# Cross-attention with folded key and value matrices, and rewritten passes of the conv mixer, in an eight-core decoder trunk

## The reference

```python
D_MODEL = 1024; BATCH = 16; SEQ = 2048; DEPTH = 2; MEM_LEN = 256
HGRN_HEADS = 8; CONV_WIDTH = 31; XATTN_HEADS = 4; XATTN_DIM = 256; D_FF = 2816

def conformer_conv_mixer(h, w_in, b_in, dw, dw_b, ln_g, ln_b, w_out, b_out):
    a, gate = jnp.split(h @ w_in + b_in, 2, axis=-1)
    u = a * jax.nn.sigmoid(gate)
    u = lax.conv_general_dilated(u, dw[:, None, :], ...) + dw_b   # depthwise, causal, width 31
    u = jax.nn.silu(layer_norm(u, ln_g, ln_b))
    return u @ w_out + b_out

def memory_cross_attention(h, mem_n, wq, wkv, wo):
    q = (h @ wq).reshape(B, S, XATTN_HEADS, XATTN_DIM)
    k, v = jnp.split(mem_n @ wkv, 2, axis=-1)
    s = jnp.einsum('bshd,bmhd->bhsm', q, k).astype(jnp.float32) * (XATTN_DIM ** -0.5)
    p = jax.nn.softmax(s, axis=-1).astype(v.dtype)
    o = jnp.einsum('bhsm,bmhd->bshd', p, v).reshape(B, S, D)
    return o @ wo

def reference(...):
    mem_n = rms_norm(mem, mem_norm)                      # shared by both layers
    h = x
    for layer in range(DEPTH):
        h = h + 0.5 * swiglu_ffn(rms_norm(h, ffn1_norm[layer]), ffn1_w_in[layer], ffn1_w_out[layer])
        hn = rms_norm(h, mix_norm[layer])
        h = h + (hgrn2_mixer(hn, ...) if layer == 0 else conformer_conv_mixer(hn, ...))
        h = h + memory_cross_attention(rms_norm(h, xattn_norm[layer]), mem_n, xattn_wq[layer], xattn_wkv[layer], xattn_wo[layer])
        h = h + 0.5 * swiglu_ffn(rms_norm(h, ffn2_norm[layer]), ffn2_w_in[layer], ffn2_w_out[layer])
    return rms_norm(h, final_norm)
```

## Time and profile before

| | |
|---|---|
| median of 3 runs | 6222.91 us (6216.97 to 6978.02) |
| the profiled execution, its time | 6235.01 us |
| its span, slowest core (core 4) | 6233.5 us |
| spans of the eight cores | 6202.5 to 6233.5 us |
| mean granted TensorE clock, core 4 | 0.962 |

### The profile page before, as it was taken

One profiled execution on the slowest core, in us unless ns is written; L12 is line 12 of the kernel. 1 busy time (PEld: TensorE's weight loads), 2 busy tenths in 40 slices (PEclk: granted clock), 3 DMA queues, 4 the chain that ended last, 5 costly groups with the idle time before them and its releaser, 6 DMA issues.

```text
span 6233.5 us, 88931 instructions; the slowest of 8 cores (6202.5 to 6233.5 us)
## 1 busy us (share of the span) xinstructions
PE 5689.4 (91%) x31032; PEld 2786.8 (45%) x31600; DVE 3170.8 (51%) x4054; ACT 2118.9 (34%) x3223; POOL 965.9 (15%) x828
## 2 busy tenths in 40 slices
PE   8899988999999867899989999889999998688999
PEld 3345543444444444344444455434444445443443
DVE  4336565544534556644553465564344445656434
ACT  3118883211311344311331288632122122543113
POOL 2102440000000441000000034200000014400000
PEclk9999999999999988999999999999999999899998
...
GB/s 127 53 26 25 27 26 57 54 34 41 47 33 10 38 45 75 24 48 35 94 103 32 27 26 27 49 47 41 41 40 44 30 6 46 45 65 38 31 31 55
DMA packets 442111, 271.58 MB, mean 44 GB/s; under 512 B 179280, under 2 KB 404560, under 8 KB 441680
## 3 DMA queue, kind: packets, MB, share of 16 engines
...
## 4 chain that ended last, share of the span: by engine, by line
PE 82%; issue 6%; DVE 5%; ACT 3%; DMA 2%; POOL 2%; SPq 1%; DVEq 0%; ACTq 0%; POOLq 0%
PE ps L646 38%; PE ps L661 19%; PE ps L753 4%; PE ps L740 4%; PE ps L1005 3%; PE ps L855 3%; PE ps L957 2%; PE ps L566 2%; PE ps L1094 2%; DVE hn_tok L562 1%; PE ps L883 1%; PE ps L1026 1%; DVE arena L776 1%; PE ps L766 1%; DMA arena<-conv_dw 1%
## 5 line engine op out<-in xcount | busy, mean ns | idle before, releaser
L646 PE MATMUL ps<-arena 128*128 128x512 bf16 x11021 | 2498.8, 383 | 29.6 <-DVE arena L776 10.5
L646 PEld LDWEIGHTS ps<-arena 128*128 128x128 bf16 x11264 | 1107.2, 99 | 1360.0 <-issue 102.1
L649 DVE TENSOR_TENSOR arena<-ps,arena 128x512 bf16<-128x512 f32 x704 | 486.3, 691 | 1801.4 <-PE ps L646 1776.4
L648 ACT ACTIVATE arena<-ps 128x512 bf16<-128x512 f32 x704 | 420.0, 597 | 2754.5 <-PE ps L646 2739.3
L661 PE MATMUL ps<-arena 128*128 128x512 bf16 x5516 | 1255.1, 381 | 14.8 <-DVE h L663 5.7
L663 DVE SCALAR_TENSOR_TENSOR h<-ps,h 128x512 f32<-128x512 f32 x1536 | 1044.1, 689 | 229.8 <-PE ps L661 223.5
L661 PEld LDWEIGHTS ps<-arena 128*128 128x128 bf16 x5632 | 550.5, 98 | 685.0 <-issue 55.2
L593 POOL DMA_DIRECT2D arena<-ffn_w_in x176 | 154.9, 884 | 2407.8 <-PE ps L646 1862.4
L538 ACT ACTIVATE junk<-h 128x1024 bf16<-128x1024 f32 x288 | 303.5, 1054 | 332.9 <-DVE h L596 198.0
L1005 PE MATMUL ps<-arena 128*128 128x512 bf16 x1475 | 368.0, 386 | 3.2 <-issue 0.2
L562 DVE SCALAR_TENSOR_TENSOR hn_tok<-h,stat,gB 128x1024 bf16<-128x1024 f32 x256 | 359.4, 1451 | 20.4 <-PE ps L566 15.1
...
## 6 DMA issues: line engine op xcount, KB each, us to landing
arena<-ffn_w_in POOLq DMA_DIRECT2D x176, 512.0 KB, 8.9
arena<-ffn_w_out POOLq DMA_DIRECT2D x88, 512.0 KB, 6.9
...
y<-arena SPq DMA_DIRECT2D x32, 512.0 KB, 3.5
h<-x SPq DMA_DIRECT2D x20, 512.0 KB, 6.3
...
```

The source lines that it names most:

```text
L646: P.op("pe", lambda e, bb=bb, ga=ga, k=k, j=j: e.matmul(psb(bb), lhsT=wiv[:, ga, k, j * 128:(j + 1) * 128], rhs=hnT[:, k, blk * 512:(blk + ...
L648: P.op("act", lambda e, bg=bg, j=j: e.activation(out=sg[j].ap, in_=psb(bg), func=AF.Silu), reads=psk(bg), writes=sg[j].keys())
L649: P.op("dve", lambda e, bu=bu, j=j, q=q: e.tensor_tensor(out=actv[:, q, :], in0=psb(bu), in1=sg[j].ap, op=ALU.mult), reads=psk(bu) + sg[j] ...
```

## The change

The scores (h Wq)(M Wk)^T of a head are h times a 1024x256 matrix Wq (M Wk)^T, and the output P (M Wv) Wo is P times a 256x1024 matrix. Both matrices depend on layer, sequence and head alone. They are now made once, for both layers and both sequences, in 16 steps (`fold_steps`) recorded at steps 7 to 22 of the very first feed-forward, whose rings shrink from 5 and 5 slots to 3 and 4; they are written to HBM as bf16 through SP's queue and read back by each cross-attention. A step for keys has 4 x 8 matmuls of 256 columns that project the memory, 16 transposes of Wq and 32 matmuls of 256 columns; a step for values has 32 matmuls of 256 columns and 16 of 512. Cross-attention then goes by tiles of 128 tokens: `weigh` (16 matmuls of 512 columns, tokens on partitions, row maximum by `tensor_reduce`, four Exp with bias and sum, one product with the reciprocals), and two tiles later `mix` (8 transposes of the weights, a ScalarE copy, 16 matmuls of 512 columns). `middle` is recorded after step 4, once, for both sequences' memory tokens; the vectors come in rows and are transposed, and the depthwise weights in one load.

In the conv mixer the right operand of the projections is read with a step of 4 tokens, so that the VectorE operation writes without a step; bands and the bias on `h` move from POOL to VectorE; the statistics are split in three; all four classes are scaled on VectorE; and a product with a shifted selection matrix `spread` (32 matmuls of 512 columns a block) takes the place of the 32 transposes and interleaves the classes, so that the copies out of PSUM are contiguous, half on ScalarE, half on VectorE.

```diff
+        P.op("pe", lambda e: e.transpose(out=ps[:, P.place[bv], 0:40], in_=vrow[0:40, :], identity=identf[0:40, 0:40]), reads=vrow_buf.keys() + [("vrow", i) for i in range(4)] + idf_buf.keys(), writes=psk(bv))
...
+            P.op("pool", lambda e: e.dma_start(out=dwtok, in_=cv_dw_d[0]), reads=["tick"], writes=dwtok_buf.keys(), dma=True)
+            P.op("dve", lambda e: e.tensor_copy(out=dwrep, in_=dwtok.rearrange("p (g c) -> p g c", c=32)[:, :, None, :].to_broadcast([CW, D // 32, 4, 32])), reads=dwtok_buf.keys(), writes=dwrep_buf.keys())
...
-            NW, NO, NA = 5, 5, 3
+            NW, NO, NA = (5, 5, 3) if middle is None else (3, 4, 3)
...
-            for g in range(1, NW):
+            for g in range(1, max(NW, NO)):
-                load_wi(g, late)
+                if g < NW:
+                    load_wi(g, late)
...
-                if middle is not None and i == 2 * NB:
+                if middle is not None and i == 4:
                     middle()
+                if steps and i >= 7:
+                    steps.pop(0)()
...
-        def emit_xattn(layer, hook):
...
+        def mem_norms():
...
+        def fold_steps(fw, wqT, kvT, st):
...
+            def project(s, scale):
+                for j in range(2):
+                    for k in range(KC):
+                        P.op("pe", lambda e, k=k, j=j: e.matmul(ps[:, P.place[b], j * 256:(j + 1) * 256], lhsT=wkv_[0][:, k, j * 128:(j + 1) * 128], rhs=mv[:, k, :], start=(k == 0), stop=(k == KC - 1)),
+                P.op("act", lambda e: e.activation(out=kvv[s], in_=psb(b).rearrange("p (j m) -> p j m", m=MEM), func=AF.Copy, scale=scale), reads=psk(b), writes=kvT[s].keys())
...
+            def keys_step(l, hh):
+                wload(wkv_[0], xa_wkv_d[l][:, hh * 256:(hh + 1) * 256].rearrange("(k p) n -> p k n", p=128), fw[0].keys())
+                wload(wkv_[1], xa_wq_d[l][:, hh * 256:(hh + 1) * 256].rearrange("(k p) n -> p k n", p=128), fw[1].keys())
+                for s in range(NSEQ):
+                    project(s, float(256 ** -0.5))
+                for j in range(2):
                     b = P.bank()
                     for k in range(KC):
+                        P.op("pe", lambda e, k=k, j=j, b=b: e.transpose(out=psb16(b)[:, k * 128:(k + 1) * 128], in_=wkv_[1][:, k, j * 128:(j + 1) * 128], identity=ident[:]), reads=fw[1].keys() + ["ident"], writes=psk(b))
...
+                                P.op("pe", lambda e, k=k, i=i, j=j, b=b, s=s: e.matmul(ps[:, P.place[b], i * 256:(i + 1) * 256], lhsT=wqTv[:, j, k * 128:(k + 1) * 128], rhs=kvv[s][:, j, :], start=(j == 0), stop=(j == 1)),
...
+                    P.op("sp", lambda e, s=s, sv=sv: e.dma_start(out=fa_d[l, s, :, :, hh * 256:(hh + 1) * 256], in_=sv), reads=st[s].keys(), writes=[("fa", l, s, hh)], dma=True)
...
+            def values_step(l, hh):
+                wload(wkv_[0], xa_wkv_d[l][:, D + hh * 256:D + (hh + 1) * 256].rearrange("(k p) n -> p k n", p=128), fw[0].keys())
+                wload(wov, xa_wo_d[l][hh * 256:(hh + 1) * 256, :].rearrange("(j p) n -> p j n", p=128), fw[1].keys())
+                for s in range(NSEQ):
+                    project(s, 1.0)
...
+                                P.op("pe", lambda e, mt=mt, half=half, j=j, b=b, s=s: e.matmul(psb(b), lhsT=kvv[s][:, j, mt * 128:(mt + 1) * 128], rhs=wov[:, j, half * 512:(half + 1) * 512], start=(j == 0), stop=(j == 1)),
...
+                    P.op("sp", lambda e, s=s, sv=sv: e.dma_start(out=fv_d[l, s, :, 2 * hh:2 * hh + 2, :], in_=sv), reads=st[s].keys(), writes=[("fv", l, s, hh)], dma=True)
+            return [lambda l=l, hh=hh, f=f: f(l, hh) for l in range(2) for hh in range(4) for f in (keys_step, values_step)]
...
+        def emit_xattn(layer, sq, hook):
+            offs = ((0, 42, 58), (16, 32, 48))[layer]
+            A = ABuf(arena, HNT_B + offs[0] * 1024, KC * D, BF16)
+            VW = ABuf(arena, HNT_B + offs[1] * 1024, KC * D, BF16)
+            CV.off = HNT_B + offs[2] * 1024
+            ex = [CV.take(D, F32) for _ in range(2)]
+            pn = [CV.take(D, BF16) for _ in range(3)]
+            pT = [CV.take(D, BF16) for _ in range(3)]
...
+            for k in range(0, KC, 4):
+                P.op("sp", lambda e, k=k: e.dma_start(out=Av[:, k:k + 4, :], in_=fa_d[layer, sq, :, k:k + 4, :]), reads=[("fa", layer, sq, hh) for hh in range(4)], writes=A.keys(k * D, (k + 4) * D), dma=True)
...
+            def weigh(tt):
+                x, z = tt % 2, tt % 3
+                exv = ex[x].ap.rearrange("p (h m) -> p h m", m=MEM)
+                for hf in range(2):
+                    for k in range(KC):
+                        P.op("pe", lambda e, k=k, hf=hf, b=b: e.matmul(psb(b), lhsT=hnT[:, k, tt * 128:(tt + 1) * 128], rhs=Av[:, k, hf * 512:(hf + 1) * 512], start=(k == 0), stop=(k == KC - 1)),
+                    P.op("dve", lambda e, hf=hf, b=b: e.tensor_reduce(out=xst[:, z, 0, 2 * hf:2 * hf + 2], in_=psb(b).rearrange("p (h m) -> p h m", m=MEM), op=ALU.max, axis=AX.X, negate=True), reads=psk(b), writes=[("xmax", z, hf)])
+                    for i in range(2):
+                        hh = 2 * hf + i
+                        P.op("act", lambda e, hh=hh, i=i, b=b: e.activation(out=exv[:, hh, :], in_=ps[:, P.place[b], i * 256:(i + 1) * 256], func=AF.Exp, bias=xst[:, z, 0, hh:hh + 1], accum_out=xst[:, z, 1, hh:hh + 1]),
+                P.op("dve", lambda e: e.reciprocal(out=xst[:, z, 2, :], in_=xst[:, z, 1, :]), reads=[("xsum", z, hh) for hh in range(4)], writes=[("xrec", z)])
+                P.op("dve", lambda e: e.tensor_tensor(out=pn[z].ap.rearrange("p (h m) -> p h m", m=MEM), in0=exv, in1=xst[:, z, 2, :, None].to_broadcast([128, 4, MEM]), op=ALU.mult), reads=ex[x].keys() + [("xrec", z)], writes=pn[z].keys())
...
+            def mix(tt):
+                for i in range(KC):
+                    P.op("pe", lambda e, i=i, b=b: e.transpose(out=psb16(b)[:, i * 128:(i + 1) * 128], in_=pn[z].ap[:, i * 128:(i + 1) * 128], identity=ident[:]), reads=pn[z].keys() + ["ident"], writes=psk(b))
+                P.op("act", lambda e, b=b: e.activation(out=pT[z].ap, in_=psb16(b), func=AF.Copy), reads=psk(b), writes=pT[z].keys())
+                    for i in range(KC):
+                        P.op("pe", lambda e, i=i, half=half, bo=bo: e.matmul(psb(bo), lhsT=pT[z].ap[:, i * 128:(i + 1) * 128], rhs=VWv[:, i, half * 512:(half + 1) * 512], start=(i == 0), stop=(i == KC - 1)),
+                    add_to_h(tt, half, bo)
+            for tt in range(NT + 2):
+                if tt < NT:
+                    weigh(tt)
+                if tt >= 2:
+                    mix(tt - 2)
+                    if (tt - 2) % 4 == 3:
+                        hook((tt - 2) // 4)
...
+            def y_of(b, q):
+                if q == 0:
+                    return y
+                return ABuf(arena, HNT_B + (b * 4 + (0, 0, 0, 1)[q]) * 4096 + (0, 0, 2048, 0)[q], D, BF16)
...
-                P.op("pool", lambda e: e.tensor_tensor(out=h[:, tt, :], in0=h[:, tt, :], in1=gB[:, gn, :], op=ALU.add), reads=[("h", tt), ("gB", gn)], writes=[("h", tt)])
+                P.op("dve", lambda e: e.tensor_tensor(out=h[:, tt, :], in0=h[:, tt, :], in1=gB[:, gn, :], op=ALU.add), reads=[("h", tt), ("gB", gn)], writes=[("h", tt)])
...
-                            P.op("pe", lambda e, bb=bb, a=a, k=k, v=v, blk=blk: e.matmul(psb(bb), lhsT=v[:, a, k, :], rhs=hnT[:, k, blk * 512:(blk + 1) * 512], start=(k == 0), stop=(k == KC - 1)),
+                            P.op("pe", lambda e, bb=bb, a=a, k=k, v=v, blk=blk: e.matmul(psb(bb), lhsT=v[:, a, k, :], rhs=hnT[:, k, blk * 512:(blk + 1) * 512].rearrange("p (t q) -> p q t", q=4), start=(k == 0), stop=(k == KC - 1)),
...
-                    P.op("dve", lambda e, ba=ba, s=s, c=c, blk=blk: e.scalar_tensor_tensor(out=uTv[:, :, blk * 128:(blk + 1) * 128].rearrange("p q t -> p t q"), in0=psb(ba).rearrange("p (t q) -> p t q", q=4), scalar=vecs[:, V_BA, c:c + 1], in1=sg[s].ap.rearrange("p (t q) -> p t q", q=4), op0=ALU.add, op1=ALU.mult),
+                    P.op("dve", lambda e, ba=ba, s=s, c=c, blk=blk: e.scalar_tensor_tensor(out=uTv[:, :, blk * 128:(blk + 1) * 128], in0=psb(ba).rearrange("p (q t) -> p q t", q=4), scalar=vecs[:, V_BA, c:c + 1], in1=sg[s].ap.rearrange("p (q t) -> p q t", q=4), op0=ALU.add, op1=ALU.mult),
...
-                P.op("pool", lambda e: e.tensor_tensor(out=v, in0=mask32[:, None, :].to_broadcast([128, 36, 32]), in1=dwS[:, gi, :, None].to_broadcast([128, 36, 32]), op=ALU.mult),
+                P.op("dve", lambda e: e.tensor_tensor(out=v, in0=mask32[:, None, :].to_broadcast([128, 36, 32]), in1=dwS[:, gi, :, None].to_broadcast([128, 36, 32]), op=ALU.mult),
...
+            cuts = (0, 512, 768, D)
...
-                if c == 5:
+                if c in (3, 5):
                     for b in range(NB):
-                        stats(b, 0)
+                        stats(b, c // 5)
...
-                for q in (2, 0, 3, 1):
+                for q in range(4):
...
```

(21 more changed lines are left out.)

255 lines of the change are left out of this document (98 added, 157 removed).

## The result

The changed kernel takes 0.9736 of the time of the one before, 95% interval 0.9708 to 0.9764, so it is 2.6% faster; the forecast of 6033 us against 6222.9 was a ratio of 0.9695. In some executions of either kernel the cores of one die or both are granted a lower clock and the time grows by some per cent; these make the plain medians of this comparison 6172.34 us (6055.7 to 6941.49, 4 runs) and 6481.65 us, and are left out of the ratio and of all that follows. Without them the changed kernel took 6054.45, 6055.70 and 6057.36 us; the last is the profiled execution (span 6055.7 us on core 3, clock 0.986).

What follows compares the result with a forecast made beforehand. TensorE, busy 5689 of 6233.5 us, was taken as the bound; -165 - 56 + 123 - 20 - 12 - 60 = -190 us on 6235.0 gave 6045, less 12 for the median 6033 us, range 5965 to 6150.

Steps and rivals of the forecast that it cites:

- Part 1: Cross-attention's PE work: 736 units become 512 plus 128 transposes' 7.2 us, 41.2 us less a stage, -165 us over four.
- Part 2: Cross-attention's gaps, where PE stands: 14 us a stage in place of 28, -56 us (bounds -96 to 0).
- part 5: Conv mixer's main part: contiguous VectorE write, bands and bias on VectorE shrink gaps, -12 us (-30 to +15).
- two tiles of lead: Cross-attention: two `weigh` tiles, 6.9 us, cover the chain of maximum, Exp, reciprocal and product, some 4.5 us.
- Parts 3 and 4: Fold in the first feed-forward, +123 us; depthwise weights in one load ending PE's wait, -20 us.
- Rival (c): Fold stalls the first feed-forward, each of 16 steps waiting 8.9 us for a load: +142, 6175 us; chance 0.10.
- Part 6: Conv mixer's tail: 120 us in place of 154 a sequence, -60 us for two sequences (-80 to -20).
- Part 7: Mixer projections' right operand read at a step of 8 bytes: taken at no cost, bounds 0 to +575 us.
- rival (a): Mixer projections' stepped reads are slow: sign turns above factor 1.86; at factor 2, +221 us, 6254; chance 0.10.
- (b): Gaps in attention and mixer stay, half the tail's extra PE work shows: -42 us, 6181; chance 0.12.
- (d): Attention's row maximum costs as the reciprocal, VectorE 11 us a tile: +205 us, 6238; chance 0.05.

Runs made afterwards that it cites:

- the two first runs: Changed kernel with projections' right operand read contiguously: VectorE still writing in steps, 5858 to 5864 us; then VectorE reading in steps and writing contiguously, 5828.74 us.

## Why the prediction was right or wrong

By starts of stages (HGRN2's first projection 524.3 and 634.3 us; the mixer's 2071.7 and 2085.5) and by the experiments, the sum was in fact -365 for attention, +110 for the fold with the vectors, -137 for the mixer without the stepped read, +228 for the stepped read: -164 us. Against the forecast of -190 that is +228 for the stepped read, -144 for attention, -65 for the mixer (forecast -72) and +7 for the fold. That the sum of these is only 26 us is luck.

**Part 1, attention's PE work: right.** 512 units and 256 transposes at the prices of the earlier trace rows are 125 us; the window of 130 us holds them and 20 matmuls of the feed-forward, with nothing left over.

**Part 2, attention's gaps: the term was mis-sized.** The prediction had 28 us of gaps a stage, of which half would stay. The experiments give 91 us a stage, 41 of them PE's count, so the gaps were worth 50 and all of them went. For the first stage the starts of instructions show it: from the first query matmul to the mixer the kernel before took 1142 us, and PE's work in it at full clock is 166 + 2 x 463 = 1092. Of these some 50 us, 28 are idle time in the stage's own window, which is what the prediction saw; 12 are idle time behind it, up to the mixer, and 9 stand in PE's busy time (1101 against 1092) at a mean clock of 0.99. After, it is 1051 us, against 1051 by count. Not all of it is attention's: with the conv mixer of before it is 1064, so that 13 us belong to part 5. The reason given, two tiles of lead, fell; shown is that the long reciprocal made 21 of the 50 in this stretch (1121 us without it) and 29 a stage over all four. What made the rest (the late kv weights, the smaller waits) was not taken apart stage by stage. 4 x (91 - 55) = 144 us of the error stand here.

**Parts 3 and 4, fold and vectors: right.** The first feed-forward grew by 107 us between its first projection and HGRN2's, and by 110 with the later start; the forecast was 123 - 20 = 103. PE's wait for depthwise weights is gone, the longest wait on fold weights is 1.2 us, and the smaller rings cost nothing. Rival (c) fell.

**Part 5, the mixer's main part: under-sized.** The gaps at its entry were credited to the stepped write alone. The run with POOL's bands shows 52 us for moving bands and bias, and the two first runs 31 us for the stepped write: together 83 us where the forecast had 12. (Single effects overlap: those of parts 5 and 6 add up to 154 us, and together they gave 137.) The view that would have told it is POOL's 250 us idle behind the norms, next to the norm's 1451 ns; the earlier trace rows told the same mechanism for the tail, and the prediction used it only there.

**Part 6, the tail: right in the main.** 109 us against a forecast of 120 (bounds 110 to 140), bound by the first block's 22 us, as forecast, and then by PE alone, whose only other wait there is 1.5 us; VectorE, busy for 86 of the 109, was not a bound beside it. The prediction's own count by PE, 19 + 4 x 22.5 = 109, was the time, and the 11 us on top of it were not needed. Selection matmuls -37, scaling on VectorE -34, and the split of the statistics, to which the prediction gave no price of its own, 0.

**Part 7, the stepped operand: wrong, and the step that failed.** It was priced at nothing between bounds of 0 and +575, on the two hits that it took from the Trainium skill (Advanced Engine Details and Errata, SBUF Cachelines) and on the thought that PE reads where L951 writes. Measured +228 us: rival (a), at its factor of 2, to which the prediction gave 0.10 and +221 us. Its condition for the sign, a factor of 1.86, was passed (2.1); the sign held only since part 2 and the mixer gave 209 us more than forecast. Rivals (b) and (d) fell: hardly a gap stayed, and the maximum takes 0.69 us.
